# Two of four input tiles issued from the ScalarE queue instead of the SyncE queue

## The reference

```python
hn = rms_norm(x, g_pre_mix)              # x is 512 x 1024
proj = hn @ w_in                         # then split into heads and channels
mixed = concat([moba_attention, forgetting_attention, short_conv]) @ w_out
x = x + rms_norm(mixed, g_post_mix)
h2 = rms_norm(x, g_pre_ffn)
ff = (silu(h2 @ w_gate) * (h2 @ w_up)) @ w_down
return x + rms_norm(ff, g_post_ffn)
```

## Time and profile before

| what | value |
|---|---|
| median of 3 runs | 585.87 us |
| the profiled execution's own time | 585.19 us |
| its span in the profile | 583.5 us |
| TensorE busy | 573.6 us |
| ScalarE busy | 314.6 us |
| VectorE busy | 459.5 us |
| GpSimd busy | 127.5 us |
| moved by DMA | 76.82 MB |

### The profile page before, as it was taken

How to read it: one execution, slowest core, us unless ns; L and a number is a source line. 1 busy time by engine, 2 the same in 40 slices (tenths; PEclk the granted TensorE clock), 3 DMA queues, 4 the chain that set the end, 5 groups by cost and what they waited for, 6 DMA issues and landing times.

```text
span 583.5 us, 9854 instructions
## 1 busy us (share of the span) xinstructions
PE 573.6 (98%) x3517; PEld 511.9 (88%) x3517; DVE 459.5 (79%) x740; ACT 314.6 (54%) x520; POOL 127.5 (22%) x136
## 2 busy tenths in 40 slices
PE   7999999999999999999999999999999999999996
PEld 5878888888888878899999999999999998888884
DVE  4768888888768864779888887978798678888787
ACT  7636666566544544547353544445363465547752
POOL 1111011132200010063423223242423004344100
PEclk9999999999999999999999999999999999999999
DMA  7643433334123470302232313232231449999833
GB/s 296 179 151 111 120 94 108 125 92 127 55 74 120 137 285 36 109 37 72 77 141 77 140 72 144 72 110 106 102 113 72 144 151 286 261 215 205 163 144 144
DMA packets 27322, 76.82 MB, mean 132 GB/s; under 512 B 3194, under 2 KB 3194, under 8 KB 27292
## 3 DMA queue, kind: packets, MB, share of 16 engines
q1 hardware_dynamic: 18204, 54.83, 26.8%
q0 software_dynamic: 9088, 21.61, 16.9%
HBM read 69.06 MB, written 4.22 MB: 126 GB/s over the span
## 4 chain that ended last, share of the span: by engine, by line
PE 96%; DMA 1%; DVE 1%; ACT 1%; issue 0%; SPq 0%; DVEq 0%; ACTq 0%
PE bank L1765 12%; PE bank L1764 12%; PE bank L1763 12%; PE bank L1511 11%; PE bank L1513 11%; PE bank L1512 11%; PE bank L1817 6%; PE bank L1821 6%; PE bank L1819 6%; PE bank L1645 3%; PE bank L1633 2%; PE bank L1557 2%; PE bank L1623 1%; PE bank L1621 1%; DMA x_sb<-in_x 1%; PE bank L1604 1%
## 5 line engine op out<-in xcount | busy, mean ns | idle before, releaser
L1765 PE MATMUL bank<-tok_hi,form_lo 128*128 128x256 f32 x320 | 90.6, 283 | 0.0
L1764 PE MATMUL bank<-tok_lo,form_hi 128*128 128x256 f32 x320 | 90.6, 283 | 0.0
L1763 PE MATMUL bank<-tok_hi,form_hi 128*128 128x256 f32 x320 | 90.6, 283 | 0.0
L1511 PE MATMUL bank<-hn_hi,w_hi 128*128 128x512 f32 (+2 forms) x200 | 78.8, 394 | 0.1
L1513 PE MATMUL bank<-hn_hi,w_lo 128*128 128x512 f32 (+2 forms) x200 | 77.0, 385 | 0.0
L1512 PE MATMUL bank<-hn_lo,w_hi 128*128 128x512 f32 (+2 forms) x200 | 76.8, 384 | 0.0
L1765 PE MATMUL bank<-hn_hi,form_lo 128*128 128x256 f32 x240 | 67.9, 283 | 0.0
L1764 PE MATMUL bank<-hn_lo,form_hi 128*128 128x256 f32 x240 | 67.9, 283 | 0.0
L1763 PE MATMUL bank<-hn_hi,form_hi 128*128 128x256 f32 x240 | 67.9, 283 | 0.0
L1763 PEld LDWEIGHTS bank<-tok_hi,form_hi 128*128 128x128 f32 x320 | 61.4, 192 | 0.0
L1764 PEld LDWEIGHTS bank<-tok_lo,form_hi 128*128 128x128 f32 x320 | 61.4, 192 | 0.0
(11 more groups left out here) (199 smaller groups left out, 1394.2 us busy)
## 6 DMA issues: line engine op xcount, KB each, us to landing
raw<-in_w_in_units SPq DMA_DIRECT2D x24, 512.0 KB, 3.4
raw<-in_w_gate_units SPq DMA_DIRECT2D x22, 512.0 KB, 3.3
raw<-in_w_up_units SPq DMA_DIRECT2D x22, 512.0 KB, 4.2
down_x<-in_w_down POOLq DMA_DIRECT2D x15, 512.0 KB, 11.6
down_y<-in_w_down SPq DMA_DIRECT2D x10, 512.0 KB, 11.6
raw<-in_w_out SPq DMA_DIRECT2D x8, 512.0 KB, 3.3
q_lh<-q_hl POOLq DMA_DIRECT2D x12, 256.0 KB, 2.8
down_x<-in_w_down SPq DMA_DIRECT2D x5, 512.0 KB, 4.3
```

Source lines behind the costliest of these rows:

```text
L1511: nc.tensor.matmul(out_ap, sh, mh, start=first, stop=False)
L1763: nc.tensor.matmul(out_ap, sh, mh, start=first and k == 0, stop=False, skip_group_check=True)
L1764: nc.tensor.matmul(out_ap, sh, ml, start=False, stop=False, skip_group_check=True)
L1765: mm = nc.tensor.matmul(out_ap, sl, mh, start=False, stop=k == HK - 1, skip_group_check=True)
```

## The change

The loop that issues the tiles of `x` is cut in two. SyncE issues tiles 0 and 2. ScalarE issues tiles 1 and 3, as its first two instructions, ahead of the load of its function table. Semaphores, destinations and everything that follows stay the same. No DMA was issued from ScalarE before.

```diff
@@ -463,7 +463,7 @@
-            for t in range(TT):
+            for t in range(0, TT, 2):
                 sp.dma_start(x_sb[:, t, :], x[P * t:P * (t + 1), :]).then_inc(x_in[t], 16)
             load(0, unit(w_in_units, 0))
             sp.dma_start(g_mix_c[:, :], g_pre_mix).then_inc(small_in, 16)
@@ -684,6 +684,8 @@
 
+            for t in range(1, TT, 2):
+                act_e.dma_start(x_sb[:, t, :], x[P * t:P * (t + 1), :]).then_inc(x_in[t], 16)
             nc.scalar.preload_act_table(ACT.Sqrt)
             act_e.wait_ge(consts_done, 1)
             for t in range(TT):
```

## The result

The changed kernel takes 588.09 us (median of 14 executions, 586.36 to 589.57); the kernel before, run beside it, takes 586.63 (14 executions, 585.24 to 587.73). The ratio is 1.0029, 95% interval 1.0019 to 1.0039: slower, by about 1.7 us by the ratio (the medians themselves lie 1.46 us apart). The profiled execution took 588.72 us, of which 587.0 are its span, 3.5 more than the span before.

What follows compares the result with a forecast made beforehand. TensorE, busy for 573.6 of 583.5 us, was taken as the bound, so a shift of the first projection reaches the end. Free issues plus +1.23 us from sharing, on the median 585.87, gave 587.1 us; range 585.6 to 588.3.

Steps and rivals of the forecast that it cites:

- its own sum: Whole kernel: a shift of +1.23 us on the median of 585.87, giving 587.1 us, +0.21%.
- even sharing: Tile landings: two queues share the DMA engines, each pair lands together, tile 3's squares start +1.23 us later; chance 0.52.
- The two issues on ScalarE: Start of ScalarE: two issues of 0.45 us each, covered by the wait for tile 0, cost 0.
- SyncE's earlier issues: SyncE's queue: what follows the tiles goes out 0.9 us earlier, worth nothing because the DMA engines are full.
- Rival B: Tile landings: the order is kept, 585.8 to 586.0; with ScalarE's queue first +0.6 us; chance 0.32 for both orders.
- the 3.78 us tail: From tile 3's squares to the first projection matmul: 3.78 us of untouched work, shifted whole, projection at about 14.0.
- rival C: TensorE before the projection: sharing plus a clock rising late, +0.4 to +2 us more, 587.5 to 589; chance 0.13.
- A: Tile landings: the forecast case of even sharing, +0.9 to +1.4 us, 586.8 to 587.3; chance 0.52.
- the 6.8 us of the unit issued at 22.78 us: Later DMA: a 512 KB SyncE unit meeting GpSimd's swap takes 6.8 us, against 3.3 alone; read as queues sharing.

Runs made afterwards that it cites:

- experiment 4: The kernel before with each tile cut into two halves of 64 partitions, SyncE issuing the lower and ScalarE the upper; ratio 1.007.
- experiment 7: The kernel before with only tile 1 issued from ScalarE, tiles 0, 2 and 3 from SyncE; ratio 1.0014.
- Experiment 3: The changed kernel with 24 instead of 16 idle transposes ahead of tile 0's; ratio 1.0006 to the kernel before, median 586.29 us.
- Experiment 6: The kernel before, all tiles from SyncE, with 9 instead of 16 idle transposes; ratio 1.0027.
- experiment 2: The kernel before with all four tiles issued from ScalarE and none from SyncE; ratio 1.0043.
- experiment 5: The kernel before with each tile cut into two halves of 512 columns, SyncE issuing the left and ScalarE the right; ratio 1.0013.

## Why the prediction was wrong

It gave the greater chance, 0.52, to a change within 0.2%, though its own sum lay just beyond (+0.21%), and its likeliest case, even sharing, as the whole story. The measured change is 0.29%. The size of the sum, +1.23 us, is near the measured 1.7, but by luck: its one term was too large for an ordinary execution, and the term that carries most of the loss was not in it.

**What held.** The two issues on ScalarE are free. Tiles 0 and 1 land together near 5.5 (stated 5.3 to 5.4), tiles 2 and 3 at 8.6 and 9.0 (stated 8.8 to 8.96). The squares of tile 3 start at 10.04 in the profile (stated 10.21). Everything from the projection on passes a shift through whole: 570.7 to 571.2 us in every trace. No gain from SyncE's earlier issues shows. Rival B is out: the two tiles of a pair land within 0.4 us of each other. The rule of the Trainium skill, "DMA: Bandwidth & Descriptors", section "Queues, rings and completion order", that an engine drains a packet of some 9 to 17 descriptors before it switches, would have kept the order; no trace here shows the order kept.

**The step that failed: the 3.78 us tail, and with it rival C.** The sum took the way from tile 3's squares to the projection as "work that the edit doesn't touch". In the profile after it is 16.24 - 10.04 = 6.20 us, 2.42 more, all of it work at the lower clock. I gave "TensorE's clock comes up late" a chance of 0.13, with the remark that "what follows 7.9 us is dense work again". A loss of this size fits about half of the executions: 14 of the 26 of the changed kernel took 588.5 us or more, 12 took 587.7 or less (medians 589.0 and 586.7). The pause that I had put at 6.8 to 7.9 us was 6.58 to 8.13 in the profile. That the dense work afterwards would save it was wrong. In the profile the clock did come up, in time for tile 0's transposes, and fell back after the pause, for some 7 us. Of the 14 slower executions 8 have a mean clock of 0.991 to 0.994, as the profiled ones do; the other 6 have 0.997 to 0.999, and there the clock probably rose late, as in the traces of experiments 4 and 7, but no trace of the changed kernel shows it. Experiment 3 removes the loss by filling the pause. Experiment 6 makes a loss of its size (1.0027) with the tiles where they were, but its mechanism has no trace.

The traces show two kinds. In both traces of the changed kernel, and in that of experiment 2, the 16 idle transposes took 3.37 to 3.42 us instead of 3.67: the clock had come up before the pause, and the granted clock fell to 0.50 behind it. In experiments 4 and 7 they took 3.68. There the clock had not come up before the pause, and it rose late: the projection began 1.68 and 1.09 us after it was due. The size of C, +0.4 to +2 on top of A, was a little low: 2.4 us in the profile.

**The term that was mis-sized: sharing.** Against the profiled execution of before it is +1.06 for a stated +1.23. But that execution was quick: 585.19 us, where the medians of before later were 586.0 to 586.6. I noted the 0.68 us between the profile and the median of three and added the shift on top of the median all the same. The shift is the distance between the landing of tile 2 on one queue and on two, and in four of the six traces on one queue the former is late by itself. Between the two kernels with 24 idle transposes it is 0.25 us by the medians and 0.5 by the ratios, too little for these intervals to tell from nothing.

**A reading that was weaker than stated.** The 6.8 us of the unit issued at 22.78 us were taken as a sign of sharing alone. SyncE's unit before it was issued at 21.5 and landed only at 26.1, so a part of the 6.8 is the wait behind its own queue. The conclusion held for whole tiles; the halves of experiment 4 landed 1.2 us apart.

**What stays open.** Why tile 2 is late on one queue in many executions, why the clock falls back in some executions of the changed kernel and not in others, and what sharing costs in an ordinary execution, was not settled. Nor was a longer group of the kernel before itself: 6 of its 14 executions beside the changed kernel took 587.2 us or more (up to 587.73), against 6 of 86 beside the later experiments, and none of them has a trace. No version tried beats the kernel before.

## What to carry to other kernels

Two queues with whole tiles shared the DMA engines about evenly here, so the second queue brought the first of two needed transfers later (5.5 us for 4.2) and the second no sooner: keep transfers that are consumed in order on one queue, and count what stands on the other. A delay of a microsecond where TensorE is being kept busy on purpose can cost more through the clock than through the wait; when an input moves, check whether the filler work still reaches it. A stretch of work that an edit leaves alone can still take longer, if it runs at another clock: 3.78 us became 6.20. Before adding a shift to a median, look at how far the waits that it replaces vary between executions.

## What the runs showed of the hardware

- Two transfers of 64 partitions each, side by side on two queues, moved 234 to 241 GB/s with the DMA engines full (experiment 4), and the one on ScalarE's queue landed 1.2 us ahead of its twin; the same bytes as 128 partitions of 2 KB rows moved at 351 to 383 (experiment 5).
- The column of the granted clock can read 1.00 while TensorE works at the lower level: in experiment 6 TensorE's transposes took 0.25 us each from 6.8 to 9.8 us under a column that reads 1.00, and in experiment 7 the run's mean clock is 1.000. The durations of equal instructions tell it.
- In the changed kernel's profile the granted clock fell to 0.50 at 9.6 us, after a pause of 1.54 us and a shorter one of 0.38, and came back at 16.4, although TensorE worked without a break from 9.49 on.
- Filling the pause with eight more idle transposes kept it at 1.00: tile 1's transposes took 0.88 us instead of 1.48 (experiment 3).
